# Moving an expert layer's biases on chip: gate/up biases as four 32-row matmuls, down biases once from transposed gates

## Chip, cores and metric

The kernel runs on one core of one Trainium2 chip. It is written in Bass: each engine has its own instruction list, and the lists are tied together by semaphores. The metric is the device time of one execution in microseconds (us). Engines are named as the profile names them: PE is TensorE, DVE is VectorE, ACT is ScalarE, POOL is GpSimd, and SP issues most of the DMAs (SPq is its queue of DMA issues). PEld is the weight load of TensorE, which runs beside its matmuls.

## Reference

One decoder layer is computed for 280 tokens (16 meta tokens, 256 prompt tokens, 8 running sequences): attention and pooling mixers, then a mixture of experts. The change lies in the experts alone. All numbers are float32.

```python
D_MODEL, D_FF, N_EXPERTS, TOP_K = 1024, 1024, 32, 4
SWIGLU_LIMIT, SWIGLU_ALPHA = 7.0, 1.702

def moe(h, w_router, b_router, w_gate_up, b_gate_up, w_down, b_down):
    t = h.reshape(-1, D)
    logits = (t @ w_router + b_router)
    top_v, top_i = lax.top_k(logits, TOP_K)
    gates = jax.nn.softmax(top_v, axis=-1)
    ...
    def expert_block(args):
        xb, ei = args
        gu = xb @ w_gate_up[ei] + b_gate_up[ei]
        gate = jnp.minimum(gu[:, :D_FF], SWIGLU_LIMIT)
        up = jnp.clip(gu[:, D_FF:], -SWIGLU_LIMIT, SWIGLU_LIMIT)
        act = gate * jax.nn.sigmoid(gate * SWIGLU_ALPHA)
        return ((up + 1.0) * act) @ w_down[ei] + b_down[ei]
    ...
    y = jax.ops.segment_sum(yp[dest] * g_s[:, None], tok_s, num_segments=T)
```

Every token goes to four of 32 experts, and an expert's output row, its down bias with it, is multiplied by the token's gate for that expert before it is added up.

## The kernel before

The first part of the program (mixers, output projection, router) takes about a quarter of the span and is not touched. The rest is a loop over 16 pairs of experts. A pair (`pair` in the PE, ACT and DVE lists) handles up to 64 tokens of each of its two experts (SL = 64): rows 0 to 63 of every tile belong to the first expert, rows 64 to 127 to the second. A second pass over the experts exists for the case that an expert has more than 64 tokens.

On PE a pair runs in this order:

- L922 turns the pair's gated one-hot choice `pickg` (three 128x128 transposes), which ACT copies to `pickT`.
- Four chunks c = 0..3 of gate/up matmuls (L949). A chunk is two of eight 128-row pieces of the 1024 inputs, four PSUM banks of 512 columns (banks 0 and 1 the gate, 2 and 3 the up part) and both experts e, whose 64 columns of weights fill one half of the array each: 16 matmuls in the program. One float32 matmul stands in the trace as two MATMUL records, so a chunk is 32 records there.
- After chunk 0, the gate/up biases (L960): four matmuls, one per bank, with `half[1]`, two rows of ones and zeros that say which slot belongs to which of the two experts, as weights, and the pair's two bias rows `b_gate` or `b_up` as the moving side (2 rows, 512 columns). In the trace they are 8 records.
- `gather` (L910) picks the tokens of the next pair: 24 matmuls of 128 columns.
- The down biases (L970): two matmuls with two rows, which open the accumulation in banks 0 and 1.
- L976 turns `hid`, the product of gate and up that DVE and ACT have made meanwhile (L1611 to L1620, L1212), in eight transposes; ACT and DVE copy it to `hidT`.
- Two chunks of down matmuls (L997, 32 records each).
- L1009, L1013 and L1017 multiply the result `ye` by `pickT` and so send each row back to its token with its gate; DVE adds this to `x` and `y_last` (L1626, L1629).

The weights of a pair are twelve DMAs of 2 MB, eight of `w_gate_up` and four of `w_down`, into a ring of six slots of 2 MB each (`slot`). SP issues them in order; before each it waits (L337, `load_slots`) until PE has finished the chunk that used the slot before, which the last matmul of the chunk tells by `slot_free`. Chunk c = 0, the one after it and so on each take two neighbouring slots, one per expert, so three chunks fit in the ring. Three small DMAs of 8 KB each bring the pair's bias rows (`load_gu_bias`, L351, two DMAs; `load_down_bias`, L354). For pair 0 nine of the twelve weight DMAs are issued during the first part, three of them into room that is free there (`spare`), and pair 1's first three follow as pair 0 frees slots.

The order of the work is written out by hand in each engine's list; nothing reorders it but PE's own weight loads.

The lines that issue a pair's loads and the two bias matmuls:

```python
            def load_slots(p, n, chunks):
                for c in chunks:
                    s = c % NSLOT
                    sp.wait_ge(slot_free[s], 2 * n + 1 + c // NSLOT)
                    load(p, c, slot[s], in_chunk[s])
```

## Time and profile before

| | |
|---|---|
| runs of the kernel before | 1427.12, 1435.75, 1449.08 us |
| median | 1435.75 us |
| span of the profiled execution | 1444.9 us |
| time of the profiled execution, the only one above the span | 1449.08 us |
| PE busy | 1394.6 us, 97% of the span |
| DVE, ACT, POOL busy | 312.6, 196.6, 84.6 us |
| mean granted TensorE clock | 0.921 of full speed |
| read from memory | 445.73 MB, 310 GB/s over the span |
| chain that ended last | PE 94%, DVE 3%, ACT 1%, issue 1% |

How to read it. Busy PE says only that matmuls are in flight; how fast they go is told by the granted clock (1.00 is 2.4 GHz, 0.50 is 1.2 GHz) and by the duration of a group of equal matmuls. The chain of work that ended last is followed back from the last instruction; where it stays on PE for whole pairs, the sum of PE's groups is the time. For the DMA the view of windows gives the share of the 16 DMA engines that was busy in a stretch and what they moved. SP's waits say whether transfers were held back by PE, which had not freed a slot yet.

### The profile page before, as it was taken

What the parts mean: (1) busy time and instruction counts of PE and PEld (TensorE: products, weight loads), DVE (VectorE), ACT (ScalarE), POOL (GpSimd) and SP (SyncE); (2) the same over time, 40 slices, a digit from 0 to 9 for tenths busy, and PEclk for the clock granted to TensorE, in tenths of its full rate; (3) what the DMA queues carried; (4) which work ended last, traced back from release to release, by engine and by line L of the source; (5) the groups of instructions that cost most, each with busy time, mean ns of one, the idle gap of its engine ahead of it and who ended that gap; (6) DMA issues with size and microseconds to landing.
All of it is one profiled execution on the core that took longest, in us unless ns stands there. A gap on an engine that the chain in (4) does not pass through costs nothing.

```text
span 1444.9 us, 15673 instructions
## 1 busy us (share of the span) xinstructions
PE 1394.6 (97%) x6385; PEld 652.2 (45%) x6385; DVE 312.6 (22%) x575; ACT 196.6 (14%) x333; POOL 84.6 (6%) x110
## 2 busy tenths in 40 slices
PE   6999999997999999999999999999999999999996
PEld 4757667645343443434343434434343434343432
DVE  2434365622021111111111112111111111111112
ACT  1134321210110101010101011110101011011101
POOL 4267200000000000000000000000000000000000
PEclk9999999996899998889999999998888999999987
DMA  9247450645668999999999999999998999999992
GB/s 313 85 147 235 129 197 0 252 149 215 238 243 339 369 371 369 373 369 371 390 354 374 363 377 400 403 390 374 370 373 369 372 389 388 376 367 373 367 375 84
DMA packets 92154, 447.61 MB, mean 310 GB/s; under 512 B 6298, under 2 KB 15942, under 8 KB 59221
## 3 DMA queue, kind: packets, MB, share of 16 engines
q1 hardware_dynamic: 85447, 427.35, 74.7%
q0 software_dynamic: 5632, 18.88, 4.2%
q10 hardware_dynamic: 1046, 0.97, 0.2%
q8 instruction: 21, 0.34, 0.1%
q14 instruction: 8, 0.07, 0.0%
HBM read 445.73 MB, written 1.68 MB: 310 GB/s over the span
## 4 chain that ended last, share of the span: by engine, by line
PE 94%; DVE 3%; ACT 1%; issue 1%; DMA 0%; ACTq 0%; DVEq 0%; SPq 0%
PE ps L949 33%; PE ps L997 17%; PE ps L910 10%; PE ps L960 5%; PE ps L786 4%; PE ps L970 2%; PE ps L759 2%; PE ps L1009 2%; PE ps L615 2%; PE ps L976 2%; DVE arena L1629 1%; PE ps L1017 1%; PE ps L502 1%; PE ps L633 1%; PE ps L1013 1%; PE ps L548 1%
## 5 line engine op out<-in xcount | busy, mean ns | idle before, releaser
L949 PE MATMUL ps<-arena 128*64 128x512 f32 x2048 | 481.2, 629 | 4.5 <-DVE arena L1629 4.4
L949 PEld LDWEIGHTS ps<-arena 128*64 128x64 f32 x2048 | 169.6, 145 | 312.6 <-issue 294.3
L997 PE MATMUL ps<-arena 128*64 128x512 f32 x1024 | 246.0, 642 | 1.5 <-ACT arena L1041 1.5
L1041 ACT ACTIVATE arena<-ps 128x512 f32<-128x512 f32 (+9 forms) x169 | 95.5, 583 | 515.1 <-PE ps L997 225.7
L997 PEld LDWEIGHTS ps<-arena 128*64 128x64 f32 x1024 | 76.8, 148 | 161.4 <-issue 155.1
L910 PE MATMUL ps<-arena 128*128 128x128 f32 (+1 forms) x768 | 142.7, 318 | 1.1 <-DVE arena L1591 1.1
L910 PEld LDWEIGHTS ps<-arena 128*128 128x128 f32 (+1 forms) x768 | 109.0, 195 | 44.0 <-issue 15.5
L1611 DVE TENSOR_SCALAR arena<-ps 128x512 f32<-128x512 f32 x32 | 22.1, 692 | 474.5 <-PE ps L949 474.5
L1212 ACT ACTIVATE arena<-arena 128x512 f32<-128x512 f32 x32 | 20.2, 631 | 507.6 <-DVE arena L1611 507.6
L1626 DVE TENSOR_TENSOR arena<-arena,ps 64x512 f32<-64x512 f32 x16 | 10.9, 679 | 282.3 <-PE ps L1013 282.3
L960 PE MATMUL ps<-arena 2*128 2x512 f32 x128 | 69.8, 690 | 0.0
L786 PE MATMUL ps<-arena 128*128 128x280 f32 x256 | 66.2, 414 | 0.0
L786 PEld LDWEIGHTS ps<-arena 128*128 128x128 f32 x256 | 49.0, 196 | 15.9 <-issue 4.5
L1622 DVE COPY arena<-ps 128x512 f32<-128x512 f32 x16 | 11.1, 692 | 138.9 <-PE ps L976 138.9
L960 PEld LDWEIGHTS ps<-arena 2*128 2x128 f32 x128 | 23.7, 194 | 37.2 <-issue 37.2
L1629 DVE TENSOR_TENSOR arena<-arena,ps 128x1024 f32<-128x1024 f32 x32 | 37.6, 1218 | 5.8 <-PE ps L1017 5.8
L970 PE MATMUL ps<-arena 2*128 2x512 f32 x64 | 38.0, 720 | 0.8 <-DVE arena L1611 0.8
L615 PE MATMUL ps<-arena 128*128 128x128 f32 x256 | 32.6, 276 | 2.3 <-ACT arena L1041 1.7
L421 POOL DMA_INDIRECT arena<-in_cache_ckv,arena x32 | 30.6, 955 | 58.7 <-PE ps L548 27.6
L1017 PE MATMUL ps<-arena 128*128 128x512 f32 x64 | 31.7, 618 | 0.0
L1009 PE MATMUL ps<-arena 128*128 128x512 f32 x64 | 31.7, 618 | 0.0
L759 PE MATMUL ps<-arena 128*128 128x512 f32 x64 | 31.3, 646 | 0.0
(282 smaller groups left out, 881.1 us busy)
## 6 DMA issues: line engine op xcount, KB each, us to landing
arena<-in_w_gate_up SPq DMA_DIRECT2D x128, 2048.0 KB, 11.9
arena<-in_w_down SPq DMA_DIRECT2D x64, 2048.0 KB, 12.3
arena<-in_w_in SPq DMA_DIRECT2D x8, 1024.0 KB, 9.3
arena<-in_w_out SPq DMA_DIRECT2D x2, 2048.0 KB, 11.7
arena<-in_w_in SPq DMA_DIRECT2D x2, 1088.0 KB, 11.9
arena<-in_w_in SPq DMA_DIRECT2D x1, 2048.0 KB, 23.8
arena<-in_consts SPq DMA_DIRECT2D x1, 1096.0 KB, 7.8
arena<-in_w_uq SPq DMA_DIRECT2D x1, 768.0 KB, 15.0
```

Of the source, the lines that this page charges most:

```text
L615: m = nc.tensor.transpose(ps[:, 3 * (s % 2) + k, P * i:P * i + P], key[:, P * k:P * k + P], ident)
L759: m = mm(ps[:, bank, :], mT[:, k, P * t:P * t + P], w_out[n][:, k, :], start=(k == 0), stop=(k == KD - 1))
L786: m = mm(ps[:, 4 + u, 0:T], w[:, kk, u, P * (h % 2):P * (h % 2) + P], hT[:, kk, :], start=(kk == 0), stop=(kk == KD - 1))
L910: m = mm(ps[:, 6 + k // 4, P * (k % 4):P * (k % 4) + P], h2[0:n, t, P * k:P * k + P], pick[0:n, t, :, :].rearrange("p u s -> p (u s)"), st ...
L949: m = mm(ps[SL * e:SL * e + SL, b, :], xg[:, 2 * c + kk, SL * e:SL * e + SL], w[e][:, kk, b, :], start=(c == 0 and kk == 0), stop=(c == 3 ...
L960: mm(ps[:, b, :], half[1], row[:, 512 * (b % 2):512 * (b % 2) + 512], start=False, stop=False, skip_group_check=True)
L970: mm(ps[:, u, :], half[2], b_down[:, 512 * u:512 * u + 512], start=True, stop=False, skip_group_check=True)
L997: m = mm(ps[SL * e:SL * e + SL, u, :], hidT[:, 4 * c + kk, SL * e:SL * e + SL], w[e][:, kk, u, :], start=False, stop=(c == 1 and kk == 3), ...
L1009: mm(ps[:, 2 + 2 * t, :], pickT[:, t, :], ye[:, 0:512], start=True, stop=True)
L1017: m = mm(ps[:, 3 + 2 * t, :], pickT[:, t, :], ye[:, 512:D], start=True, stop=True)
L1041: return act.activation(out, in_, ACT.Copy)
L1629: dve.tensor_tensor(x[:, t, :], x[:, t, :], ps[:, 2 + 2 * t:4 + 2 * t, :].rearrange("p b n -> p (b n)"), ALU.add).then_inc(y_added, 1)
```

## The change

Gate/up biases. All 32 experts' `b_gate_up` rows are loaded once: four DMAs put columns 512b to 512b+511 of the 32 rows into partitions 32b to 32b+31 of `bias`. DVE writes for each pair a tile `whose` (128x128; `name_slots`, a copy of two columns of the constant `eye32`, each repeated over 64 slots), which holds in each group of 32 partitions the same one-hot matrix from expert to slot. Four matmuls (L932 of the changed kernel), one per bank, take 32 rows of `whose` as weights and 32 rows of `bias` as the moving side: bank b uses the partitions 32b to 32b+31. They stand ahead of chunk 0 and open the accumulation there. The four two-row matmuls after chunk 0 are gone.

Down biases. The sum over a token's experts of gate times down bias is `gates` times `b_down`. PE turns the gates once (`turn_gates`, three matmuls), ACT copies them to `gatesT` (32x384), and in pair 0 alone six matmuls (32 rows) with all 32 rows of `b_down` open the six accumulations of L1009, L1013 and L1017. The two matmuls of L970 and their wait are gone from every pair, and the down matmuls open banks 0 and 1 themselves.

Loads. The 48 bias DMAs of 8 KB each are replaced by five (four of 64 KB and one of 128 KB) in the first part, in the place in SP's list where `final_g` (512 KB) was loaded; `final_g` goes behind pair 1's loads, into a spare slot.

```diff
@@ -200,19 +200,22 @@
         xg = at(norm2_start + SLOT, KD * P).rearrange("p (k s) -> p k s", k=KD)
         y_last = at(take(512), 512)[0:64, :]
 
-        b_gate, b_up, b_down = x[32:34, 2, :], xn[32:34, 2, :], xn[64:66, 2, :]
+        b_down = xn[64:64 + NE, 2, :]
+        gatesT = x[64:64 + NE, 2, 0:NT * P]
         assert 4 * D + NT * P <= 2 * KD * T
         gate, sgm, up = (at(hT0 + D * j, D) for j in range(3))
         hidT = at(hT0 + 3 * D, D).rearrange("p (j n) -> p j n", j=KD)
         hid, ye = up, gate
 
-        final_g = at(norm2_start + SLOT + KD * P, D)
+        start = norm2_start + SLOT + KD * P
+        bias = at(start, 512)
+        whose = at(start + 512, P)
         spare = [at(take(SLOT), SLOT), at(norm2_start, SLOT), at(take(SLOT), SLOT)]
-        assert norm2_start + SLOT + KD * P + D <= con0 + sum(n for _, n in FRONT)
+        final_g = spare[2][:, 0:D]
+        assert start + 512 + P <= con0 + sum(n for _, n in FRONT)
         top[0] = max(top[0], top_front)
 
         ident = const["ident"]
-        half = [const["half"][r:r + 2, :] for r in (0, 32, 64)]
 
 
 
@@ -344,43 +348,32 @@
                     sp.wait_ge(slot_free[s], 2 * n + 1 + c // NSLOT)
                     load(p, c, slot[s], in_chunk[s])
 
-            def load_gu_bias(p, n):
-
-                sp.wait_ge(slot_free[0], 2 * n + 1)
-                for dst, col in ((b_gate, 0), (b_up, D)):
-                    sp.dma_start(dst, a["b_gate_up"][0, bass.ds(2 * p, 2), col:col + D]).then_inc(in_bias, 16)
-
-            def load_down_bias(p):
-                sp.dma_start(b_down, a["b_down"][0, bass.ds(2 * p, 2), :]).then_inc(in_b_down, 16)
-
             def pair_weights(p, n):
-                load_gu_bias(p, n)
-                load_slots(p, n, range(NSLOT))
-                load_down_bias(p)
-                load_slots(p, n, range(NSLOT, 2 * NSLOT))
-
-
-
-            load_gu_bias(0, 0)
+                load_slots(p, n, range(2 * NSLOT))
+
+
+
             load_slots(0, 0, range(4))
             sp.wait_ge(pe_wo, 2)
             sp.wait_ge(out_small, 176)
             load(0, 6, spare[0], in_wo[0])
-            sp.dma_start(final_g, a["final_norm_g"].rearrange("(a n) -> a n", a=1).to_broadcast([P, D])
-                         ).then_inc(in_final, 16)
+
+            for b in range(4):
+                sp.dma_start(bias[32 * b:32 * b + NE, :], a["b_gate_up"][0, :, 512 * b:512 * b + 512]
+                             ).then_inc(in_bias, 16)
+            sp.dma_start(b_down, a["b_down"][0, :, :]).then_inc(in_bias, 16)
             load_slots(0, 0, range(4, 6))
             load(0, 8, spare[2], in_p)
             sp.wait_ge(top_ready, 1)
             load(0, 7, spare[1], in_wo[1])
-            load_down_bias(0)
             for c in range(3):
                 sp.wait_ge(slot_free[c], 2)
                 load(1, c, slot[c], in_chunk[c])
             load_slots(0, 0, range(9, 12))
-            load_gu_bias(1, 1)
-            load_slots(1, 1, range(3, NSLOT))
-            load_down_bias(1)
-            load_slots(1, 1, range(NSLOT, 2 * NSLOT))
+            load_slots(1, 1, range(3, 2 * NSLOT))
+
+            sp.dma_start(final_g, a["final_norm_g"].rearrange("(a n) -> a n", a=1).to_broadcast([P, D])
+                         ).then_inc(in_final, 16)
             with sp.Fori(2, NP) as p:
                 pair_weights(p, p)
             sp.wait_ge(most_ready, 1)
@@ -901,6 +894,13 @@
 
             pe.sem_inc(pe_comb, 1)
 
+            def turn_gates():
+
+                pe.wait_ge(pickg_ready, 1)
+                for t in range(NT):
+                    m = mm(ps[64:64 + NE, 4, P * t:P * t + P], gates[:, t, :], ident, start=True, stop=True)
+                m.then_inc(pe_rank, 1)
+
             def gather(count):
 
                 pe.wait_ge(pick_ready, count)
@@ -924,6 +924,12 @@
                 m.then_inc(pe_pick, 1)
 
                 pe.wait_ge(y_added, 3 * n + 2)
+                pe.wait_ge(whose_ready, n + 1)
+                if first:
+                    pe.wait_ge(in_bias, 80)
+                for b in range(4):
+                    q = slice(32 * b, 32 * b + NE)
+                    mm(ps[:, b, :], whose[q, :], bias[q, :], start=True, stop=False, skip_group_check=True)
                 for c in range(4):
                     s0 = 2 * (c % 3)
                     w = []
@@ -947,28 +953,17 @@
                     for j, (kk, b) in enumerate(order):
                         for e in range(2):
                             m = mm(ps[SL * e:SL * e + SL, b, :], xg[:, 2 * c + kk, SL * e:SL * e + SL],
-                                   w[e][:, kk, b, :], start=(c == 0 and kk == 0),
+                                   w[e][:, kk, b, :], start=False,
                                    stop=(c == 3 and kk == 1), skip_group_check=True)
                             if j == 7:
                                 m.then_inc(slot_free[s0 + e], 1)
                         if c == 3 and j == 3:
                             m.then_inc(pe_gu, 1)
-                    if c == 0:
-                        pe.wait_ge(in_bias, 32 * n + 32)
-                        for b in range(4):
-                            row = b_gate if b < 2 else b_up
-                            mm(ps[:, b, :], half[1], row[:, 512 * (b % 2):512 * (b % 2) + 512], start=False,
-                               stop=False, skip_group_check=True)
                 if ahead:
                     pe.wait_ge(pickT_ready, n + 1)
                     pe.wait_ge(y_added, 3 * n + 1)
                     gather(n + 2)
 
-                pe.wait_ge(gate_ready, 2 * n + 2)
-                pe.wait_ge(in_b_down, 16 * n + 16)
-                for u in range(2):
-                    mm(ps[:, u, :], half[2], b_down[:, 512 * u:512 * u + 512], start=True, stop=False,
-                       skip_group_check=True)
                 pe.wait_ge(y_added, 3 * n + 3)
                 for u in range(2):
                     pe.wait_ge(hid_ready, 2 * n + u + 1)
@@ -995,7 +990,7 @@
                     for j, (kk, u) in enumerate(order):
                         for e in range(2):
                             m = mm(ps[SL * e:SL * e + SL, u, :], hidT[:, 4 * c + kk, SL * e:SL * e + SL],
-                                   w[e][:, kk, u, :], start=False, stop=(c == 1 and kk == 3),
+                                   w[e][:, kk, u, :], start=(c == 0 and kk == 0), stop=(c == 1 and kk == 3),
                                    skip_group_check=True)
                             if j == 7:
                                 m.then_inc(slot_free[s0 + e], 1)
@@ -1005,19 +1000,30 @@
                 pe.wait_ge(pickT_ready, n + 1)
                 pe.wait_ge(ye_ready, 2 * n + 1)
                 pe.wait_ge(hid_ready, 2 * n + 2)
+                if first:
+
+                    pe.wait_ge(e_top, 2)
                 for t in range(2):
-                    mm(ps[:, 2 + 2 * t, :], pickT[:, t, :], ye[:, 0:512], start=True, stop=True)
+                    if first:
+                        mm(ps[:, 2 + 2 * t, :], gatesT[:, P * t:P * t + P], b_down[:, 0:512], start=True, stop=False)
+                    mm(ps[:, 2 + 2 * t, :], pickT[:, t, :], ye[:, 0:512], start=not first, stop=True)
                 pe.wait_ge(ye_ready, 2 * n + 2)
                 pe.wait_ge(xg_ready, n + (2 if ahead else 1))
                 for u in range(2):
+                    if first:
+                        mm(ps[32 * u:32 * u + 32, 6, :], gatesT[:, 2 * P:2 * P + 32],
+                           b_down[:, 512 * u:512 * u + 512], start=True, stop=False)
                     m = mm(ps[32 * u:32 * u + 32, 6, :], pickT[:, 2, 0:32], ye[:, 512 * u:512 * u + 512],
-                           start=True, stop=True)
+                           start=not first, stop=True)
                 m.then_inc(pe_comb, 1)
                 for t in range(2):
-                    m = mm(ps[:, 3 + 2 * t, :], pickT[:, t, :], ye[:, 512:D], start=True, stop=True)
+                    if first:
+                        mm(ps[:, 3 + 2 * t, :], gatesT[:, P * t:P * t + P], b_down[:, 512:D], start=True, stop=False)
+                    m = mm(ps[:, 3 + 2 * t, :], pickT[:, t, :], ye[:, 512:D], start=not first, stop=True)
                     m.then_inc(pe_comb, 1)
 
             gather(1)
+            turn_gates()
             pair(0, False, True, first=True)
             with pe.Fori(1, NP - 1) as p:
                 pair(p, False, True)
@@ -1225,6 +1231,8 @@
             act.wait_ge(rank_ready, 1)
             act.wait_ge(out_small, 176)
             take_gathered(1)
+            act.wait_ge(pe_rank, 2)
+            copy(gatesT, ps[64:64 + NE, 4, 0:NT * P]).then_inc(e_top, 1)
             with act.Fori(0, NP - 1) as p:
                 pair(p, False, True)
             pair(NP - 1, False, False)
@@ -1594,12 +1602,19 @@
                 dve.tensor_tensor(pickg, pick, gates[:, :, experts].unsqueeze(3).to_broadcast([P, NT, 2, SL]),
                                   ALU.mult).then_inc(pickg_ready, 1)
 
+            def name_slots(experts):
+
+                dve.tensor_copy(whose.rearrange("p (u s) -> p u s", u=2),
+                                const["eye32"][:, experts].unsqueeze(2).to_broadcast([P, 2, SL])
+                                ).then_inc(whose_ready, 1)
+
             def pair(p, n, extra, first, ahead):
                 if ahead:
                     dve.wait_ge(pe_gather, n + 1)
                     dve.wait_ge(pe_pick, n + 1)
                     choose(bass.ds(2 * p + 2, 2), n + 2, first)
                 if extra:
+                    name_slots(bass.ds(2 * p, 2))
                     choose(bass.ds(2 * p, 2), n + 1, first)
 
                 for u in range(2):
@@ -1621,6 +1636,8 @@
                 dve.wait_ge(pe_hidT, 2 * n + 2)
                 dve.tensor_copy(hidT[:, 4:8, :], ps[:, 5, :].rearrange("p (j n) -> p j n", j=4)
                                 ).then_inc(hidT_dve, 1)
+                if ahead:
+                    name_slots(bass.ds(2 * p + 2, 2))
                 dve.wait_ge(y_added, 3 * n + 3)
                 dve.wait_ge(pe_comb, 3 * n + 2)
                 dve.tensor_tensor(y_last, y_last, ps[0:64, 6, :], ALU.add).then_inc(y_added, 1)
@@ -1633,6 +1650,7 @@
 
             dve.sem_inc(y_added, 3)
             choose(slice(0, 2), 1, slice(0, SL))
+            name_slots(slice(0, 2))
             link(dve.tensor_reduce(most[0:1, 0:1], ps[0:1, 5, NT * NE:NT * NE + NE], AX.X, ALU.max))
             dve.tensor_copy(most_i[0:1, 0:1], most[0:1, 0:1]).then_inc(most_ready, 1)
             with dve.Fori(0, NP - 1) as p:
@@ -1705,7 +1723,7 @@
     put("rope0", np.concatenate([cos, cos, sin, sin, np.zeros((NO, T))]))
     put("fold", (row % R == np.arange(P) % R) & (row < 2 * R))
     put("fold_hi", (row % R == np.arange(P) % R) & (row >= NO))
-    put("half", (row % 32 < 2) & (np.arange(P) // SL == row % 32))
+    put("eye32", row % 32 == np.arange(NE))
     put("before", row < np.arange(P))
     put("iota", np.arange(PASSES * SL) + 1)
     put("mask1", np.where(np.arange(2 * P) <= P + row, 0.0, NEG))
```

On PE the two places of the loop over pairs look as follows. In these rows L949 and L955 are the gate/up matmuls of before and of the change, L960 the old and L932 the new bias matmuls; a row with x15 stands for the other fifteen matmuls of its chunk. PE, start of a pair, before:

```order
L926 ISA
L942 REGISTER_ALU [waits y_added]
L949 MATMUL ps<-arena 64x512 [waits in_chunk1,in_chunk0]
L949 MATMUL ps<-arena 64x512 x15
L957 REGISTER_ALU
L960 MATMUL ps<-arena 128x512 [waits in_bias]
L960 MATMUL ps<-arena 128x512 x3
L934 REGISTER_ALU [waits in_chunk2]
L949 MATMUL ps<-arena 64x512 [waits in_chunk3]
```

PE, the same place in the changed kernel:

```order
L926 ISA
L932 MATMUL ps<-arena 128x512 [waits whose_ready,y_added]
L932 MATMUL ps<-arena 128x512 x3
L948 REGISTER_ALU
L955 MATMUL ps<-arena 64x512 [waits in_chunk1,in_chunk0]
L955 MATMUL ps<-arena 64x512 x15
L940 REGISTER_ALU [waits in_chunk2]
L955 MATMUL ps<-arena 64x512 [waits in_chunk3]
```

The bias matmuls have moved from behind chunk 0 to ahead of it, the wait on `in_bias` has left the loop, and a wait on DVE's `whose_ready` has come. PE, between the gather (L910) and the transposes of `hid` (L976, in the changed kernel L971), before:

```order
L910 MATMUL ps<-arena 128x128 [waits pick_ready]
L910 MATMUL ps<-arena 128x128 x23
L967 ISA
L968 ISA [waits gate_ready]
L970 MATMUL ps<-arena 128x512 [waits in_b_down]
L970 MATMUL ps<-arena 128x512
L972 REGISTER_ALU
L974 REGISTER_ALU [waits y_added]
L976 MATMUL ps<-arena 128x128 [waits hid_ready]
```

PE, the same place in the changed kernel:

```order
L910 MATMUL ps<-arena 128x128 [waits pick_ready]
L910 MATMUL ps<-arena 128x128 x23
L967 REGISTER_ALU
L969 ISA [waits y_added]
L971 MATMUL ps<-arena 128x128 [waits hid_ready]
L971 MATMUL ps<-arena 128x128 x3
```

The two down-bias matmuls and the waits on `gate_ready` and `in_b_down` have gone, and nothing stands in their place.

## Rows read from the trace of the kernel before

**Rows 1.** Waits of SP from 430 to 1370 us: who waited for whom, total, times, longest.

```profile
SPq L337 <- PE ps L949: 407.9, 42, 13.1
SPq L337 <- PE ps L997: 336.2, 28, 19.1
```

**Rows 2.** Waits of PE in the same stretch.

```profile
PE ps L949 <- DVE arena L1629: 4.4, 14, 0.3
```

**Rows 3.** Chain that ended last, in order of time: start us, us, what.

```profile
365.12 9.06 PE ps L949 x32
...
430.88 7.09 PE ps L949 x32
...
910.19 3.63 PE ps L960 x8
...
913.82 20.75 PE ps L949 x96
...
1078.73 2.31 PE ps L970 x3
...
1103.82 7.09 PE ps L949 x32
...
1110.90 4.71 PE ps L960 x8
...
1115.61 23.01 PE ps L949 x96
...
1147.12 1.45 PE ps L970 x3
...
1169.25 7.14 PE ps L949 x32
...
1369.86 7.09 PE ps L949 x32
```

**Rows 4.** Windows: stretch, length, busy us of each engine, PEclk, DMA share, GB/s.

```profile
430.00:1370.00 940.00, 934.21 (x3856) 380.37 (x3856) 142.18 (x198) 98.59 (x127) 0.00 (x0) 0.92 0.93 374
1098.00:1122.00 24.00, 23.69 (x77) 8.12 (x77) 4.06 (x5) 3.65 (x4) 0.00 (x0) 0.86 1.01 424
1160.00:1220.00 60.00, 59.43 (x259) 24.91 (x257) 10.10 (x14) 7.02 (x9) 0.00 (x0) 0.97 1.00 407
1079.00:1086.00 7.00, 7.00 (x19) 2.88 (x19) 0.69 (x1) 1.51 (x2) 0.00 (x0) 0.51 1.01 417
1111.00:1113.00 2.00, 2.00 (x5) 0.86 (x6) 0.00 (x0) 0.00 (x0) 0.00 (x0) 1.00 1.02 426
1113.00:1120.00 7.00, 7.00 (x16) 1.90 (x16) 0.00 (x0) 0.00 (x0) 0.00 (x0) 0.52 1.01 421
1150.00:1212.00 62.00, 61.43 (x277) 25.67 (x275) 9.95 (x15) 6.88 (x10) 0.00 (x0) 1.00 0.99 397
```

**Rows 5.** DMA issues of the page: issues, KB each, median us to landing.

```profile
arena<-in_w_gate_up SPq DMA_DIRECT2D x128, 2048.0 KB, 11.9
arena<-in_w_down SPq DMA_DIRECT2D x64, 2048.0 KB, 12.3
```

**Rows 6.** Groups: line, operation, shapes, count | busy us, mean ns | idle before.

```profile
L960 PE MATMUL ps<-arena 2*128 2x512 f32 x128 | 69.8, 690 | 0.0
...
L1626 DVE TENSOR_TENSOR arena<-arena,ps 64x512 f32<-64x512 f32 x16 | 10.9, 679 | 282.3 <-PE ps L1013 282.3
```

**Rows 7.** Timeline of one pair: start us, us, engine, line, operation.

```profile
1098.29 1.99 PE L1009 MATMUL ps<-arena 128*128 128x512 f32 x4
...
1100.21 1.05 PE L1013 MATMUL ps<-arena 128*32 128x512 f32 x4
...
1146.59 0.69 PE L970 MATMUL ps<-arena 2*128 2x512 f32 x1
...
1146.79 0.27 PE L910 MATMUL ps<-arena 24*128 24x128 f32 x1
```

**Rows 8.** Waits of PE over the whole span.

```profile
PE ps L922 <- ACT arena L1041: 1.2, 1, 1.2
```

More of the change, by code:

```diff
@@ L56 @@
          ("diag", NB * H), ("headsel", H), ("mod32", 1), ("block", 4))
-for _name, _n in FRONT + (("ident", P), ("half", P), ("before", P), ("iota", PASSES * SL), ("valid", NT)):
+for _name, _n in FRONT + (("ident", P), ("eye32", NE), ("before", P), ("iota", PASSES * SL), ("valid", NT)):
     CONST[_name] = (_at, _n)
@@ L227, in build @@
         in_chunk = [sem(f"in_chunk{c}") for c in range(NSLOT)]
-        in_bias, in_b_down = sem("in_bias"), sem("in_b_down")
+        in_bias = sem("in_bias")
         out_small, out_y = sem("out_small"), sem("out_y")
@@ L274, in build @@
             sem(n) for n in ("pick_ready", "pickg_ready", "pe_gather", "xg_ready"))
+        whose_ready = sem("whose_ready")
         pe_gu, gate_ready, up_ready, sgm_ready, hid_ready = (
```

## Prediction

> **What bounds the kernel now.** Start with the chain that ended last. Through the loop over pairs it lies on PE from the first matmul of one pair to the first of the next: the pairs start at 365.12, 430.88, ..., 1103.82, 1169.25, ..., 1369.86 [rows 3]. The fourteen pairs from 430.88 to 1369.86 took 938.98 us, 67.07 each. PE waits for almost nothing there: 4.4 us in 14 times, for DVE's addition [rows 2]. So what PE issues in a pair is the pair's time.
>
> Next ask how fast PE goes. In the windows the granted clock of 430 to 1370 us is 0.92 [rows 4], and the short windows show that this is a mean of two levels: 1.00 (2.4 GHz) and 0.51 (1.2 GHz) [rows 4]. The matmuls of L960 that start at 1110.90 run at 1.00 until about 1113, and then the clock is half until 1120. The other window at half, 1079 to 1086, begins just after an L970 block starts, at 1078.73 [rows 3, 4]. Both places are two-row bias matmuls. Not each of them is followed by a fall: from 1150 to 1212, with the next pair's start (1169.25) and so its L960 in it, the clock stays at 1.00 [rows 3, 4]. A pair at full clock is worked out from the one that took 65.43 us (1103.82 to 1169.25): its L960 block took 4.71 against 3.63 at full clock, and the three chunks behind it 23.01 against 20.75 [rows 3]. Without these 3.34 us the pair is 62.1 us. The mean pair of 67.07 is thus 5.0 us of half clock on top of 62.1.
>
> Last come the transfers. SP waits for slots that PE has not freed: 407.9 and 336.2 us in 940 [rows 1]. So PE holds the DMA back, not the reverse. But there is little room: a pair loads twelve chunks of 2,048 KB (8 of w_gate_up and 4 of w_down, since 128 and 64 were issued for 16 pairs [rows 5]), which is 25.17 MB, and the DMA is busy for 0.93 of the stretch at 374 GB/s [rows 4]. While its queue is full it moves 424 GB/s (a stretch of w_gate_up) and 407 GB/s (60 us with both kinds in it) [rows 4].
>
> **The change part by part.**
>
> Removed, L960: eight records in a pair, 3.63 us at full clock [rows 3]. All of it lies on the chain, with PE idle 0.0 us before it [rows 6].
>
> Removed, L970: four records. In the chain three of them are 1.45 us [rows 3]; the first one starts at 1146.59, while the last of L910 is still running (1146.79) [rows 7]. I take 1.45. The transposes behind it then wait for `hid` and no longer for the bias matmuls. DVE and ACT make `hid` during the gather, so nothing comes late in place of L970, except in the last pair, which has no gather.
>
> Added, L932: four matmuls of 32 rows, eight records. The trace has no four of them in different row groups and banks. From below, two facts speak for their running side by side: L970's first record, which has its weights in rows 64 and 65, started at 1146.59 while L910's matmuls of 24 rows (1146.79) had not ended [rows 7], and L1013's four records, which use different columns, took 1.05 us in place of the 1.99 us that L1009's four full ones took [rows 7]. So two rounds cost about 1.05 us. From above they cost what eight records one after another cost, 3.63 us. A gain below nothing is excluded, since instructions are only added here. I take 1.05, the value of the nearest row. The Trainium skill, "TensorE: Matmul & The Clock Gate", section "Measured speedup vs the span model", gives 3.07 times for four row groups of 32 at 512 columns; by that the block would be an estimated 1.18 us, which no run here shows yet. What waits behind L932 is the whole chunk 0. It waits for `y_added`, as L949 did before, and for `whose_ready`. DVE writes `whose` ahead of its wait for L1013, where it sits idle 282.3 us in 16 times [rows 6]; a copy of 128 columns costs it less than the 0.68 us of the larger addition there [rows 6]. So this wait costs nothing; without that cover it would be up to 0.7 us.
>
> PE's own time for a pair becomes 62.1 - 3.63 - 1.45 + 1.05 = 58.1 us. That the clock stays at full speed is taken from where the falls were: beside the two-row matmuls, which are gone. The stretch 1150 to 1212 at 1.00 also holds that pair's gather [rows 4].
>
> Transfers then decide. At 424 GB/s for the 16.78 MB of gate/up weights (39.6 us) and 407 for the 8.39 MB of down weights (20.6 us) a pair's loads take 60.2 us, more than PE's 58.1. The bounds are 59.4 us (all at 424) and 61.8 us (all at 407). The loop becomes bound by the DMA, and PE waits about 2 us in each pair for weights. Of the expected gain of 9 us this gives 2 back. It also hides L932 up to about 3.1 us. The 48 small bias DMAs go; they hold 0.4 MB in all, 1 us at 400 GB/s over the whole loop, so I count 0.
>
> Once, in pair 0: four full-width matmuls and two of 32 columns more. L1009 has two full-width matmuls in 1.99 us [rows 7], so four are 4.0, and the two narrow ones are 1.05 like L1013 [rows 7]; with some change of shapes I take 5.5 us. `turn_gates` (three matmuls) lies where PE waited 1.2 us for ACT's copy [rows 8]; if it lasts longer it costs under 1 us. From pair 0 the two removed blocks less L932 also come off, 4.0 us, so pair 0 gets 1.5 us longer. The five new loads stand in SP's list where 512 KB of `final_g` stood and are smaller, so the first part is as before: 0.
>
> Sum: the profiled span is 1444.9 us. Fourteen pairs and the last one go from 67.07 to 60.2: 15 x 6.87 = 103.1 less; pair 0 adds 1.5. That makes a span of 1343.3. The profiled execution's time was 1449.08, 4.2 above its span, so the forecast is 1347.5, rounded to 1347 us. The median before, 1435.75, is 13 us below the profiled execution; as the half-clock stretches, which can differ from run to run, are gone in the forecast, I do not shift it.
>
> **The rivals.**
>
> *Clock falls remain.* The gather and the transposes still stand in a row, PE now has gaps while it waits for weights, and the two-row matmuls may not have been the cause alone. A half-clock stretch is some 6.8 us long (1113 to 1120 at 0.52 [rows 4]) and costs half of that, 3.4 us. With one in a pair PE needs 61.5 us, which is above the DMA's 60.2: 15 x 1.3 = 20 more, 1367 us. With two, 64.9: 15 x 4.7 = 70 more, 1417 us. Against it: the windows at half begin at the removed matmuls.
>
> *The row groups run one after another.* Then L932 costs 3.63, PE needs 60.7 us, and with the ring of three chunks the pair is about 61: 15 x 0.8 = 12 more, 1359 us. The overlap of L970 with L910 speaks against it.
>
> *The transfers are already at their limit*, so that PE's gain turns into waits. For it: the DMA's share of 0.93. If 374 GB/s [rows 4] were all there is, a pair would be 67.3 us, and the time stays at the median, 1436. Against it: 24 us at 424 GB/s, and SP's waits [rows 1, 4]. The Trainium skill, "DMA: Bandwidth & Descriptors", section "Where 436 GB/s comes from", names about 358 GB/s as the memory's share per core; that would be an estimated 70.3 us a pair. The trace does not agree: 374 GB/s over 940 us and 424 in the best stretch [rows 4].
>
> *Slower: waiting for weights keeps the clock low.* If PE, waiting in each pair, falls to half clock and stays there for much of the next chunks, each us at half costs 0.5. A pair is slower than 67.07 from the point where more than 2 x (67.07 - 58.1) = 18 us of it are at half. At 24 us it would take 70.1, and the time 1347 + 15 x 9.9 = 1496 us. In the loop of before the mean pair loses 5.0 us to half clock, which is 10 us of it; 24 would be more than twice that, with the two-row matmuls gone.
>
> **How the numbers follow.** Forecast 0.58, falls remain 0.26, one after another 0.08, transfers at the limit 0.05, slower 0.03. The forecast's own range is 1335 to 1371 (15 pairs at 59.4 or 61.8). The range for 8 in 10 goes down to 1325, for the 10 us by which the runs before differ from their median, and up to 1398, which takes in the serial case and the half of the clock case up to about 1.5 falls in a pair. About 2% is what a measurement can tell from no change, so faster means under 1407: the forecast, the serial case and 0.23 of the clock case make 0.89. Same is the transfers' case and the rest of the clock case, 0.08; slower 0.03.
>
> **What would show it.** Right: L932 x8 about 1 us in the chain; the granted clock of the loop near 1.00; PE waits for w_gate_up or w_down, 1 to 2 us in a pair, and the DMA share near 1.00 from 430 us on; SP's waits for L949 and L997 smaller. Wrong: windows at 0.5 with no two-row matmul near; L932 near 3.6 us; a DMA share of 1.00 at a rate well under 407 GB/s; or pairs of 58 us, with the DMA faster than any long stretch of before.

## The result, and the profile after

| | before | after |
|---|---|---|
| median | 1435.95 us (4 runs, 1427.12 to 1449.08) | 1343.19 us (4 runs, 1342.39 to 1347.07) |
| ratio, 95% interval | 1 | 0.9367 (0.9338 to 0.9397) |
| profiled execution, its span | 1449.08 us, 1444.9 us | 1343.23 us, 1341.3 us |

The changed kernel is 6.3% faster; the forecast was 1347 us. The profiled execution of before is the slowest of its four runs, 13 us above their median. The page of the changed kernel, its span and the sections on the span in slices and on the chain:

```profile
span 1341.3 us, 15487 instructions
...
PEclk9989999999599999999999999999999999999998
DMA  9248670345295999999999999999999999999992
GB/s 316 70 135 234 182 248 4 137 198 212 114 363 201 386 422 414 421 414 414 418 417 420 414 421 414 422 415 419 417 416 420 414 422 414 421 415 418 418 415 109
...
PE 77%; DMA 16%; DVE 3%; ACT 2%; issue 1%; SPq 1%; ACTq 0%; DVEq 0%
```

From the fifteenth slice on, the DMA is full and moves 414 to 422 GB/s, and the chain, 94% PE in the page of before, now has 16% of DMA in it. The chain of the changed kernel in order of time (start us, us, what):

```profile
360.14 1.42 PE ps L901 x6
...
362.40 1.94 PE ps L932 x8
...
428.27 1.07 PE ps L932 x8
429.34 27.62 PE ps L955 x128
...
485.97 1.14 PE ps L932 x8
...
548.00 1.14 PE ps L932 x8
549.14 7.03 PE ps L955 x31
...
556.89 15.11 DMA arena<-in_w_gate_up
572.14 8.78 PE ps L955 x32
...
609.93 1.14 PE ps L932 x8
...
632.37 7.09 PE ps L955 x32
...
1270.94 1.14 PE ps L932 x8
...
1293.55 22.96 DMA arena<-in_w_down
1316.64 7.09 PE ps L992 x32
```

These rows answer to [rows 3]. In the loop L932 takes 1.07 to 1.14 us where L960 took 3.63 to 4.71 (pair 0's L932 took 1.94), and L970 has no successor. The first pair behind pair 0 (428.27 to 485.97, 57.70 us) is still PE's alone: its four chunks run 27.62 us without a gap. From the next pair on the chain goes through a load of w_gate_up before the last chunk. The thirteen pairs from 485.97 to 1270.94 took 784.97 us, 60.38 each. Waits of the changed kernel from 430 to 1270 us (who waited for whom: total us, times, longest), PE's first, then SP's, then one of SP's before, from 430 to 1370 us, which [rows 1] leaves out:

```profile
PE ps L955 <- DMA arena<-in_w_gate_up: 24.1, 14, 2.9
```

```profile
SPq L341 <- PE ps L955: 412.6, 55, 19.8
SPq L341 <- PE ps L992: 288.1, 28, 15.8
```

```profile
SPq L351 <- PE ps L949: 75.7, 14, 5.8
```

PE now waits 24.1/13 = 1.9 us for weights in each of the thirteen pairs, where [rows 2] had only a wait for DVE. SP's waits are 700.7 of 840 us, 83%. Before they were 819.8 of 940, 87%: the 744.1 of [rows 1] and the 75.7 that SP waited for a slot ahead of a pair's gate/up biases. So their share has hardly changed. The windows (stretch, length, busy us of PE, PEld, DVE, ACT, POOL, then PEclk, DMA share, GB/s), to be read beside [rows 4]:

```profile
430.00:1270.00 840.00, 809.66 (x3781) 332.76 (x3778) 140.53 (x208) 96.71 (x125) 0.00 (x0) 0.99 1.01 413
994.00:1010.00 16.00, 16.00 (x86) 9.67 (x86) 5.34 (x8) 1.26 (x2) 0.00 (x0) 1.00 1.03 410
1014.00:1030.00 16.00, 15.87 (x69) 5.34 (x65) 1.98 (x3) 1.24 (x3) 0.00 (x0) 1.00 1.01 422
568.00:573.00 5.00, 2.75 (x14) 0.84 (x12) 0.00 (x0) 0.00 (x0) 0.00 (x0) 0.94 1.01 412
573.00:577.00 4.00, 4.00 (x16) 1.51 (x14) 0.00 (x0) 0.00 (x0) 0.00 (x0) 0.65 1.03 411
577.00:750.00 173.00, 168.73 (x799) 69.67 (x796) 30.68 (x45) 21.07 (x27) 0.00 (x0) 1.00 1.02 417
```

In the loop the clock went from 0.92 to 0.99 and the rate from 374 to 413 GB/s at a full DMA. The stretches of one kind give 410 GB/s (w_down) and 422 (w_gate_up). What is left of half clock is short: in 568 to 573 PE stands idle for 2.25 us waiting for weights, the clock is low in 573 to 577, and it is 1.00 again for the next 173 us. The last chunk takes 8.78 us there in place of 7.09; four of the thirteen pairs have such a last chunk.

The spans differ by 103.6 us: 2.7 before pair 0 (362.40 for 365.12), 96.3 in the fourteen pairs to 1270.94 (842.67 for 938.98 us), 4.7 from there to the end (70.4 for 75.1), and 0.1 given back in pair 0.

### The profile page after: what moved, and what is told of

Read it like the earlier page. It is cut to its first block, busy times and chain, and to the rows that moved or that the text cites. A ratio compares the mean times of both kernels' runs of the same rounds, so it can differ in the third digit from the quotient of the medians.

```text
span 1341.3 us, 15487 instructions
## 1 busy us (share of the span) xinstructions
PE 1261.5 (94%) x6339; PEld 602.0 (45%) x6339; DVE 314.8 (23%) x591; ACT 197.0 (15%) x334; POOL 84.6 (6%) x110
## 4 chain that ended last, share of the span: by engine, by line
PE 77%; DMA 16%; DVE 3%; ACT 2%; issue 1%; SPq 1%; ACTq 0%; DVEq 0%
PE ps L955 20%; PE ps L992 16%; DMA arena<-in_w_gate_up 14%; PE ps L910 11%; PE ps L779 5%; PE ps L1009 2%; PE ps L752 2%; PE ps L608 2%; DMA arena<-in_w_down 2%; DVE arena L1646 1%; PE ps L932 1%; PE ps L1022 1%; PE ps L495 1%; PE ps L1016 1%; PE ps L626 1%; PE ps L541 1%
## 5 line engine op out<-in xcount | busy, mean ns | idle before, releaser
L955 PE MATMUL ps<-arena 128*64 128x512 f32 x2048 | 454.6, 602 | 27.6 <-DMA arena<-in_w_gate_up 27.6
L955 PEld LDWEIGHTS ps<-arena 128*64 128x64 f32 x2048 | 153.3, 139 | 327.6 <-issue 327.6
L992 PE MATMUL ps<-arena 128*64 128x512 f32 x1024 | 223.5, 594 | 6.0 <-ACT arena L1047 4.8
L1047 ACT ACTIVATE arena<-ps 128x512 f32<-128x512 f32 (+10 forms) x170 | 96.0, 582 | 456.2 <-PE ps L992 205.9
L910 PE MATMUL ps<-arena 128*128 128x128 f32 (+1 forms) x768 | 142.7, 318 | 1.1 <-DVE arena L1599 1.1
L992 PEld LDWEIGHTS ps<-arena 128*64 128x64 f32 x1024 | 74.6, 137 | 144.5 <-issue 144.0
L910 PEld LDWEIGHTS ps<-arena 128*128 128x128 f32 (+1 forms) x768 | 109.0, 195 | 44.0 <-issue 15.5
L779 PEld LDWEIGHTS ps<-arena 128*128 128x128 f32 x256 | 48.2, 193 | 15.4 <-issue 4.5
L1022 PE MATMUL ps<-arena 128*128 128x512 f32 x64 | 32.0, 620 | 0.0
L1009 PE MATMUL ps<-arena 128*128 128x512 f32 x64 | 32.0, 620 | 0.0
L608 PEld LDWEIGHTS ps<-arena 128*128 128x128 f32 x256 | 27.8, 140 | 6.9 <-issue 4.7
L416 POOL DMA_INDIRECT arena<-in_cache_krope,arena x32 | 30.2, 944 | 9.8 <-issue 9.8
L1491 DVE RECIPROCAL arena<-arena 128x560 f32<-128x560 f32 x8 | 29.2, 3652 | 0.3
```

What stands on the lines that cost most here:

```text
L416: pool.indirect_dma_start(cache_r[u][:, 4 * R * s:4 * R * s + 4 * R], None, cache_r_rows, off).then_inc(in_cache[u], 16)
L608: m = nc.tensor.transpose(ps[:, 3 * (s % 2) + k, P * i:P * i + P], key[:, P * k:P * k + P], ident)
L779: m = mm(ps[:, 4 + u, 0:T], w[:, kk, u, P * (h % 2):P * (h % 2) + P], hT[:, kk, :], start=(kk == 0), stop=(kk == KD - 1))
L910: m = mm(ps[:, 6 + k // 4, P * (k % 4):P * (k % 4) + P], h2[0:n, t, P * k:P * k + P], pick[0:n, t, :, :].rearrange("p u s -> p (u s)"), st ...
L955: m = mm(ps[SL * e:SL * e + SL, b, :], xg[:, 2 * c + kk, SL * e:SL * e + SL], w[e][:, kk, b, :], start=False, stop=(c == 3 and kk == 1), s ...
L992: m = mm(ps[SL * e:SL * e + SL, u, :], hidT[:, 4 * c + kk, SL * e:SL * e + SL], w[e][:, kk, u, :], start=(c == 0 and kk == 0), stop=(c == ...
```

## Experiments

Two questions were asked: is the DMA what now bounds a pair, and were the two-row matmuls the cause of the lower clock? Each ratio compares a kernel with runs of before on the same chip.

### Half of each chunk's bytes

The changed kernel, which from pair 2 on loads half of each chunk (`part` is 2) and computes on with what the slot holds.

```diff
-    sp.dma_start(dst.rearrange("p (k n) -> p k n", k=count),
-                 rows[:, bass.ds((2 * p + c % 2) * KD + k, count), :])
+    sp.dma_start(dst.rearrange("p (k n) -> p k n", k=count)[:, 0:count // part, :],
+                 rows[:, bass.ds((2 * p + c % 2) * KD + k, count // part), :])
```

> The changed kernel with only half of each weight chunk loaded from pair 2 on (the other half of a slot holds old weights, so the result is not the reference's). Theory (the DMA bounds the loop now): PE no longer waits for weights, a pair takes PE's own 57.8 us, less 2.6 us for 14 pairs: 1343 - 36 = 1307 us. Rival (PE bounds it and the waits are a by-product): 1335 to 1343 us.

Measured: 1305.58 us (1304.43 to 1311.94), ratio 0.9105 (0.904 to 0.917). Its chain, one pair, and the window of its loop:

```profile
717.65 1.14 PE ps L932 x8
718.79 27.62 PE ps L955 x128
...
756.20 13.95 PE ps L992 x64
...
775.42 1.14 PE ps L932 x8
```

```profile
430.00:1270.00 840.00, 831.31 (x3932) 336.89 (x3934) 148.39 (x219) 99.53 (x130) 0.00 (x0) 1.00 0.59 225
```

With the DMA at 0.59 of its time, a pair takes 57.77 us, all of it PE's, at a clock of 1.00. So PE's own pair is 57.8 us, the forecast's 58.1 held, and 13 x (60.38 - 57.77) = 34 of the 38 us between this run and the changed kernel are what the DMA takes back in the thirteen pairs.

### The four bias matmuls in one row group

The four matmuls of L932 read rows 32 to 63, one after another; `bias` lies in two tiles there.

```diff
-    q = slice(32 * b, 32 * b + NE)
-    mm(ps[:, b, :], whose[q, :], bias[q, :], start=True, stop=False, ...)
+    mm(ps[:, b, :], whose[32:64, :], bias[b // 2][:, 512 * (b % 2):512 * (b % 2) + 512], ...)
```

> The changed kernel with the four gate/up bias matmuls all in one row group (partitions 32 to 63, bias rows of 1024 columns), so that they cannot run side by side. Theory (four row groups do run side by side, and the loop is bound by the DMA at 60.4 us a pair): the block goes from 1.1 us to about 3.6 us, PE needs 57.8 + 2.5 = 60.3 us a pair, as much as the DMA, so PE's waits for w_gate_up nearly vanish and the time rises by only 5 to 20 us, to 1348 to 1363. Rival (the loop is still bound by PE): 15 x 2.5 = 38 us more, 1381.

Measured: 1386.06 us (1385.57 to 1390.02), ratio 0.9663 (0.9598 to 0.9728), above what the theory and the rival said. L930 is L932 there and L954 is L955. The chain and two windows:

```profile
810.47 3.70 PE ps L930 x8
814.17 29.31 PE ps L954 x128
```

```profile
810.00:814.00 4.00, 3.88 (x12) 1.51 (x10) 2.58 (x4) 3.06 (x3) 0.00 (x0) 1.00 1.01 420
814.00:818.00 4.00, 4.00 (x13) 1.18 (x13) 0.00 (x0) 0.00 (x0) 0.00 (x0) 0.57 1.02 424
818.00:870.00 52.00, 51.67 (x248) 21.18 (x244) 6.17 (x10) 3.97 (x6) 0.00 (x0) 1.00 1.00 404
```

Two things are to be seen. The block takes 3.70 us in one row group and 1.14 in four: the matmuls of the changed kernel do run side by side. And behind the block, which PE ends at full clock, stands a half-clock stretch that costs 29.31 - 27.62 = 1.69 us (27.62 is the same 128 records in the changed kernel); PE does not wait for the DMA anywhere in this loop. So in this kernel a low clock follows matmuls of 32 rows too, if they run one after another in one row group. The theory as I had it, "two-row matmuls", was too narrow.

### A block put in by itself: two rows, and all rows

Behind chunk 0 the changed kernel gets four more matmuls, which add zeros to the four banks. In the first kernel they read two rows, in the second 128; they have the same columns, the same place and the same wait.

```diff
+    if c == 0:
+        pe.wait_ge(slot_free[1], 2 * n + 2)
+        for b in range(4):
+            mm(ps[:, b, :], x[32:34, 2, 0:P], bias[32:34, :], start=False, stop=False, ...)
```

The second has `mm(ps[:, b, :], zero, bias, ...)` in the last line, with `zero` a tile of 128 x 128 zeros.

> The changed kernel with four two-row matmuls of zero weights after chunk 0 in each pair (nothing is added to the sums), behind a wait of PE for its own chunk 0: the old block's size and place. PE's own pair is then about 57.8 + 4 = 61.8 us at full clock. Theory (two-row matmuls bring the clock down): falls to half clock return near the block, 2 to 4 us a pair, 64 to 66 us a pair and 1395 to 1425 us. Rival (the falls came from something else): clock near 1.00, 61.8 us a pair, 1343 + 15 x 1.5 = 1365.

> As the run with the two-row block, but the four matmuls have 128 rows of zero weights: as many records, as long, the same wait. Theory (it is the few rows, not the time spent): clock near 1.00 through the block, 61.8 us a pair, 1360 to 1370 us. Rival (any added block in that place, or zero weights, brings the falls): the same time as the two-row block.

Measured: two rows 1407.31 us (1406.78 to 1412.65), ratio 0.9812 (0.9744 to 0.988); 128 rows 1368.06 us (1366.57 to 1373.34), ratio 0.9525 (0.9462 to 0.9588). The chain of the kernel with two rows (L965 is the block), and the window behind the block:

```profile
825.91 3.69 PE ps L965 x8
829.61 22.45 PE ps L955 x96
```

```profile
830.00:834.00 4.00, 4.00 (x14) 1.26 (x12) 0.00 (x0) 0.00 (x0) 0.00 (x0) 0.58 1.00 424
```

The same of the kernel with 128 rows (L966 is the block, L956 the gate/up matmuls):

```profile
814.72 3.70 PE ps L966 x8
818.42 20.75 PE ps L956 x96
```

```profile
430.00:1290.00 860.00, 852.48 (x3884) 343.82 (x3884) 143.31 (x210) 97.12 (x124) 0.00 (x0) 1.00 1.00 403
```

At full clock the block costs the same 3.7 us of PE in both. Behind two rows the next chunks take 22.45 us and the clock is 0.58; behind 128 rows they take 20.75 and the clock of the whole loop is 1.00. The 39 us between the two kernels are therefore the clock's, and what differs between their blocks is the number of rows in use. Not every two-row block is followed by a fall: behind three of the fourteen in the loop (702.50, 764.21 and 1214.58) the next chunks took 20.75 us. Why those three are spared was not tried.

### Each half of the change alone

One kernel has the gate/up part alone (L932 in, L960 out, L970 and its loads as before), the other the down part alone (L970 out, all down biases added in pair 0, L960 as before).

```diff
 # gate/up part alone, against the changed kernel
+                for u in range(2):
+                    mm(ps[:, u, :], half2, b_down[:, 512 * u:512 * u + 512], start=True, stop=False,
+                       skip_group_check=True)
...
 # down part alone, against the kernel before
-                for u in range(2):
-                    mm(ps[:, u, :], half[2], b_down[:, 512 * u:512 * u + 512], start=True, stop=False,
-                       skip_group_check=True)
...
```

> The gate/up half of the change alone: L932 in place of the old block, the two-row block L970 and its loads kept. Theory: PE at full clock needs 57.8 + 1.45 = 59.2 us a pair, below the DMA's 60.4; falls to half clock stay at the gather and L970 in most pairs, up to 3.4 us each: 61 to 63 us a pair, 1355 to 1380 us. Rival (the two-row block behind the gather is short and brings no falls): 1343 to 1347 us, as fast as the whole change.

> The kernel before with the down half of the change alone: L970 gone, the two-row block L960 and its loads kept. Theory: PE at full clock needs 62.1 - 1.45 = 60.6 us a pair, the falls behind L960 stay (about 3 us a pair) and those at the gather and L970 go: 63.5 us a pair, 1343 + 15 x 3.1 = 1390 us, 3% below before. Rival (falls do not depend on the two-row blocks): 65.6 us a pair, 1421 us.

Measured: gate/up part 1353.08 us (1349.37 to 1356.09), ratio 0.9429 (0.938 to 0.9479), 2 us under the lower end that was expected; down part 1388.33 us (1385.25 to 1390.27), ratio 0.9688 (0.9648 to 0.9728). The gate/up part alone, chain and windows around L970:

```profile
772.60 1.45 PE ps L970 x3
...
775.39 15.65 PE ps L997 x64
```

```profile
772.00:775.00 3.00, 3.00 (x16) 1.53 (x14) 0.00 (x0) 0.33 (x1) 0.00 (x0) 1.00 1.03 412
775.00:779.00 4.00, 3.67 (x11) 1.21 (x12) 0.83 (x2) 1.18 (x2) 0.00 (x0) 0.61 1.03 425
```

The down part alone, chain and windows around L961, which is L960 there:

```profile
744.05 7.09 PE ps L950 x32
751.13 4.38 PE ps L961 x8
755.52 23.34 PE ps L950 x96
```

```profile
753.00:760.00 7.00, 7.00 (x17) 1.93 (x17) 0.00 (x0) 0.00 (x0) 0.00 (x0) 0.56 1.00 415
760.00:780.00 20.00, 20.00 (x93) 6.78 (x92) 3.74 (x6) 0.97 (x2) 0.00 (x0) 0.98 0.86 347
```

In the loop each kernel has falls behind the block that it keeps and nowhere else: behind L970, in ten of the fourteen pairs, the down matmuls take 15.65 us in place of 13.95 in the pair shown; behind L961, in all fourteen, the three chunks take 23.34 in place of 20.75. By the ratios the parts alone take 5.7 and 3.1% off, 8.8 together; the whole change takes 6.3%. The rest lies in the transfers: with half of the loads the change takes 9.0% off (ratio 0.9105).

### Larger pieces for the DMA

If the DMA is the bound, a layout that it reads faster must show in the time. The first kernel takes w_down in pieces of 16 KB for each partition (four neighbouring rows) in place of 4 KB, and the transposes of `hid` read every fourth column to match. The second does the same to w_gate_up (16 KB for 8), with the gather reading every second column. The third is the kernel before with both. The changed kernel ran once more beside the first two.

```diff
-    gu_rows = a["w_gate_up"].rearrange("l e (k p) n -> p (l e k) n", p=P)
-    dn_rows = a["w_down"].rearrange("l e (k p) n -> p (l e k) n", p=P)
+    gu_rows = a["w_gate_up"].rearrange("l e (q p k) n -> p (l e q) (k n)", p=P, q=4)
+    dn_rows = a["w_down"].rearrange("l e (q p k) n -> p (l e q) (k n)", p=P, q=2)
...
-    hid[:, 512 * u + P * j:512 * u + P * j + P]
+    hid[:, 512 * u:512 * u + 512].rearrange("p (m j) -> p j m", j=4)[:, j, :]
```

> The changed kernel once more, as the measure for the two layouts beside it on the same chip: 1343 us, pairs of 60.4 us, the DMA share 1.01 at 418 GB/s.

> The changed kernel with another layout of the down weights: partition p of a chunk holds four rows that follow each other in memory (16 KB in one piece in place of four of 4 KB), and the transposes of hid take every fourth column to match. Theory (the DMA's rate in w_down, 410 GB/s against 422 in w_gate_up, is what is left to gain): w_down goes to 422 GB/s or more, 8.39 MB in 19.9 us in place of 20.5, 15 x 0.6 = 9 us less, 1334 us. Rival (the piece size does not set the rate, or strided transposes cost more): 1343 or above.

> As the run with the down layout, and the gate/up weights too: two rows that follow each other (16 KB in one piece in place of two of 8 KB), with the gather taking every second column. Theory: the same rate for both kinds, at most 426 GB/s, 59.0 us a pair, 1343 - 15 x 1.3 = 1323 us at best, 1334 if pieces of 16 KB are no faster than those of 8 KB. Rival (the gather's strided weights slow L910, or pieces of 16 KB are slower): 1343 or above.

> The kernel before with the layout of both weights in 16 KB pieces and nothing of the change. Theory (before, PE is the bound and the DMA waits for slots): the faster transfers bring nothing, 1425 to 1445 us, same as before. Rival (before, the transfers already held the pairs back): about 20 us less, 1415.

Measured: the changed kernel again 1343.89 us (1343.63 to 1346.44); w_down in larger pieces 1329.74 (1326.34 to 1334.74), ratio 0.9273 (0.924 to 0.9306); both 1324.53 (1321.78 to 1328.22), ratio 0.924 (0.9209 to 0.9271); the kernel before with both 1435.49 (1427.97 to 1456.64), ratio 1.0001 (0.9971 to 1.003). The theory had said 1334 for the first and 1323 at best for the second. Windows of the loop and of a stretch in it, and PE's waits, in the kernel with both layouts:

```profile
430.00:1260.00 830.00, 817.15 (x3816) 339.71 (x3814) 142.19 (x208) 96.80 (x125) 0.00 (x0) 1.00 1.00 423
915.00:931.00 16.00, 15.66 (x74) 5.62 (x70) 3.14 (x5) 0.63 (x1) 0.00 (x0) 1.00 1.01 429
```

```profile
PE ps L959 <- DMA arena<-in_w_gate_up: 7.1, 12, 2.5
```

The loop moves 423 GB/s, PE's waits for weights fall from 24.1 to 7.1 us, and the time is 19 us under the changed kernel's, the best of the kernels that load all weights. In the kernel before, the same edit shows no gain. Its strided gather costs PE 4.6 us more there (147.3 for 142.7 us in all), so with the interval of 0.3% a gain of up to some 9 us could hide, but not one of 19. This settles both sides: before, when PE was the bound, a faster DMA was worth little or nothing; now it is worth most of what PE waited.

## Why the prediction was right

**L932.** 1.05 us was forecast, 1.07 to 1.14 came. The serial kernel shows why: 3.70 in one row group. The Trainium skill ("TensorE: Matmul & The Clock Gate", section "Measured speedup vs the span model") gives 3.07 times, which made an estimated 1.18 us. The runs, 3.70/1.14 = 3.2 times, come near it.

**L960 and L970.** Their own time went, as forecast, and nothing came late in their place in the loop. The new copy on DVE (`name_slots`, L1607) costs no wait in the loop; it is 0.22 us long, as the groups of the changed kernel show (busy us, mean ns, idle before):

```profile
L1607 DVE COPY arena<-arena 128x128 f32 (+1 forms) x16 | 3.5, 219 | 0.0
```

**The clock.** The falls went with the two-row blocks, and either part alone has falls only behind the block that it keeps. What the prediction had wrong is the rival "The row groups run one after another": priced at 1359 us by PE's time alone, it measured 1386, because a serial block of 32 rows brings the falls back. The side-by-side matmuls were thus worth more than their 2.6 us in a pair. The rival "Clock falls remain" and the slower one drew on PE's waits for weights; such a wait is indeed followed by a fall at 572, but only in four of the thirteen pairs that wait, and 0.01 of the clock is lost to it in the loop.

**Transfers decide.** 60.2 us was forecast for a pair, 60.38 came in the thirteen pairs that the DMA binds; 25.17 MB in 60.38 us are 417 GB/s. The 424 and 407 GB/s that the sum took for the two kinds of weights measured 422 and 410. That the second came so near is in part luck: 407 was the rate of a stretch with both kinds in it ([rows 4]), and w_down by itself had not been read. Only the first of the fourteen pairs ran ahead, at 57.70 us; PE found its chunks loaded. With it the mean of the fourteen is 60.19, and that it meets 60.2 so closely is luck too. The rival "transfers at their limit" rested on 374 GB/s, and that was PE's pace. The memory's share of 358 GB/s in the Trainium skill ("DMA: Bandwidth & Descriptors", section "Where 436 GB/s comes from") is passed in the loop of every kernel here that loads whole chunks: these move 374 to 423 GB/s. The 435 GB/s that the same section names as the ports' limit is above all of these, the nearest being 423 over a loop and 429 over 16 us.

**Where the sizes were off.** The terms outside these pairs missed by small amounts that partly cancel:

- Pair 0: +1.5 us was forecast, +0.1 came. The new down matmuls cost more than the 5.5 us: L1008 and the narrow L1014 do not overlap their partners as L1013 did, and from the first of them (415.62) to the next pair's start (428.27) there are 12.65 us, against 5.45 before (425.43 to 430.88), 7.2 more. But ahead of them 7.1 us came off and not the two blocks' 4.0, since pair 0 of before had half clock as well (its first chunk took 9.06 us where 7.09 is usual, its L997 15.65, now 13.95).
- The first part: 0 was forecast, -2.7 came. It lies within what differs from profile to profile: in the profiles of the ten runs made after the result pair 0 starts anywhere from 358.89 to 365.53, and in the changed kernel's second one, with the same first part, at 361.72. `turn_gates` (L901) took 1.42 us, in place of a wait of about 1.2.
- The last pair: -6.87 was forecast, 4.7 came off. I had named it as the pair without a gather but priced nothing: PE waits 2.3 us for `hid` there, and 3.4 and 1.2 us for its last weights.
- Around the span: 4.2 us was taken from the profiled execution, 1.9 came.

**What would show it.** L932 near 1 us, the clock near 1.00, waits for w_gate_up of 1 to 2 us and a full DMA all came. "SP's waits smaller" hardly did: 83% of the loop for 87%, in kernels with different bounds. The sign was a poor one: SP has to wait for a slot whether or not the DMA is still busy with loads issued earlier, so these waits do not tell the two cases apart. The step "So PE holds the DMA back" was right, but what bears it out is the rate (374 against 424 GB/s), not [rows 1], from which it was drawn.

## What to carry to other kernels

When work leaves the engine that bounds a loop, work out the next limit from bytes and the best rate that a full queue shows in the same trace, and cap the gain there; waits of the issuing engine told nothing of the room left here (87% and 83%). Small matmuls that add rows of 2 or 32 can be dearer than their time if they stand in one row group: those of 32 rows, spread over row groups and banks, took a third of the time, and no fall came behind them. Once transfers are the bound, look at their pieces again: a layout that gave nothing before gave 19 us after.

## What was not expected of the hardware

- Half clock came behind blocks with few rows in use. Blocks of four matmuls, equal in length (3.7 us at full clock) and in columns, were followed by it with 2 rows (0.58, behind eleven of the fourteen blocks of the loop) and with 32 rows in one row group (0.57), and not with 128 rows (1.00 over the loop); a fall cost 1.7 us or twice that. Four row groups of 32 side by side use 128 rows and last 1.14 us; whether it is the rows or the short time that spares the clock there was not tried.
- A wait of 2.25 us for weights at 570 was followed by a short half-clock stretch. In nine of the thirteen pairs the wait was not followed by one; why it comes at some and not at others is open and was not tried.
- The rate depends on the piece. In stretches of 16 us with a full queue it was 410 GB/s in pieces of 4 KB (w_down), 422 in pieces of 8 KB (w_gate_up) and 429 where both have 16 KB.
